# The expert layers of a two-block transformer on one core: 96 of 256 tokens by row gathers, the other 160 by dense plain-float32 matmuls

## The reference, cut to what matters

```python
def block(xc):                                   # 128 tokens; 8 heads, top 16 of 128 x 128 experts each
    q = (xc @ w_q).reshape(128, 8, 2, 128)
    sc = einsum('thpd,hpnd->thpn', q, subkeys)
    s1, i1 = top_k(sc[:, :, 0], 16); s2, i2 = top_k(sc[:, :, 1], 16)
    top, pos = top_k(all 256 sums s1 + s2, 16)
    idx = (i1 * 128 + i2 at pos)                  # 128 experts a token
    gate = softmax(top)
    act = gelu(einsum('ted,td->te', u[idx], xc))
    return einsum('te,ted->td', gate * act, v[idx])
x = layer_norm(ALPHA * x + peer_ffn(x, ...), ...)
```

## Time and profile before

| | us |
|---|---|
| median of 3 runs | 2287.73 (2286.67 to 2289.21) |
| span of the profiled execution | 2284.1 |
| TensorE busy in it | 2268.4 (99%) |
| VectorE, ScalarE, GpSimd busy | 1699.0, 1324.8, 430.5 |
| moved by DMA | 408.53 MB, mean 179 GB/s |

### The profile page before, as it was taken

How to read it: one execution, slowest core, us unless ns; L and a number is a source line. 1 busy time by engine, 2 the same in 40 slices (tenths; PEclk the granted TensorE clock), 3 DMA queues, 4 the chain that set the end, 5 groups by cost and what they waited for, 6 DMA issues and landing times.

```text
span 2284.1 us, 33324 instructions
## 1 busy us (share of the span) xinstructions
PE 2268.4 (99%) x12380; PEld 1929.4 (84%) x12380; DVE 1699.0 (74%) x3098; ACT 1324.8 (58%) x2181; POOL 430.5 (19%) x355
## 2 busy tenths in 40 slices
PE   9999999999999999999999999999999999999999
PEld 9788888888888888887788888888888888877887
DVE  7567588999975555668758898997555666877885
ACT  3454555578765554646555558776555564666554
POOL 1000233178710000000013316872000000000000
PEclk9999999999999999999999999999999999999999
DMA  7455455544455655644455554445556575333555
GB/s 257 156 176 190 161 191 189 183 167 156 149 194 193 203 193 194 231 163 142 141 171 187 193 177 169 153 155 190 194 193 232 184 227 179 135 123 118 185 186 173
DMA packets 112096, 408.53 MB, mean 179 GB/s; under 512 B 12592, under 2 KB 12640, under 8 KB 111680
## 3 DMA queue, kind: packets, MB, share of 16 engines
q1 hardware_dynamic: 107712, 391.63, 50.4%
q0 software_dynamic: 3504, 13.47, 1.7%
q10 hardware_dynamic: 720, 1.31, 0.2%
HBM read 405.30 MB, written 1.05 MB: 178 GB/s over the span
## 4 chain that ended last, share of the span: by engine, by line
PE 87%; DVE 9%; ACT 2%; issue 1%; DMA 1%; POOL 0%; ACTq 0%; DVEq 0%
PE ps L716 24%; PE ps L633 21%; PE ps L705 12%; PE ps L636 11%; PE ps L672 3%; PE ps L669 3%; PE ps L676 3%; DVE lo L1967 3%; PE ps L915 2%; PE ps L768 1%; DVE big L1973 1%; ACT hi L1373 1%; DVE big L2303 1%; PE ps L889 1%; PE ps L616 1%
## 5 line engine op out<-in xcount | busy, mean ns | idle before, releaser
L1967 DVE TENSOR_TENSOR lo<-raw,hi 128x1024 fp32r<-128x1024 f32 (+1 forms) x627 | 765.4, 1224 | 366.1 <-ACT hi L1373 363.6
L1373 ACT ACTIVATE hi<-raw 128x1024 fp32r<-128x1024 f32 x677 | 714.3, 1057 | 479.7 <-PE ps L716 270.7
L633 PE MATMUL ps<-xs,hi 128*128 128x512 f32 x2560 | 650.8, 396 | 1.0 <-DVE big L2918 1.0
L633 PEld LDWEIGHTS ps<-xs,hi 128*128 128x128 f32 x2560 | 459.2, 189 | 83.6 <-DVE big L2918 1.1
L636 PEld LDWEIGHTS ps<-xs,lo 128*128 128x128 f32 x2560 | 349.0, 190 | 25.8
L636 PE MATMUL ps<-xs,lo 128*128 128x256 f32 x2560 | 356.3, 282 | 0.0
L2998 POOL TENSOR_SCALAR lnp<-iota,selT 128x128 f32<-128x128 f32 x256 | 278.1, 1097 | 167.0 <-DVE negT L2345 88.9
L705 PE MATMUL ps<-hi,lefts 128*128 128x512 f32 x986 | 304.0, 389 | 0.0
L716 PE MATMUL ps<-lo,lefts 128*128 128x512 f32 x986 | 303.7, 389 | 0.0
L716 PE MATMUL ps<-hi,lefts 128*128 128x512 f32 x986 | 303.6, 389 | 0.0
L716 PEld LDWEIGHTS ps<-hi,lefts 128*128 128x128 f32 x986 | 184.9, 188 | 38.7 <-DVE lefts L2033 0.2
(11 more groups left out here) (370 smaller groups left out, 2505.8 us busy)
## 6 DMA issues: line engine op xcount, KB each, us to landing
raw<-in_peer_u SPq DMA_DIRECT2D x256, 512.0 KB, 3.2
raw<-in_peer_v SPq DMA_DIRECT2D x256, 512.0 KB, 4.2
raw<-in_ret_vg SPq DMA_DIRECT2D x32, 512.0 KB, 3.2
raw<-in_peer_q SPq DMA_DIRECT2D x24, 512.0 KB, 3.2
raw<-in_ffn_up SPq DMA_DIRECT2D x22, 512.0 KB, 3.3
raw<-in_ffn_down SPq DMA_DIRECT2D x22, 512.0 KB, 4.0
raw<-in_ffn_gate SPq DMA_DIRECT2D x18, 512.0 KB, 4.3
raw<-in_ret_qk SPq DMA_DIRECT2D x16, 512.0 KB, 4.6
```

Source lines behind the costliest of these rows:

```text
L633: e.matmul(out, uh[:, k, :], xs[:, k, :, :].rearrange("p h t -> p (h t)"), start=k == 0, stop=False)
L1373: e.activation(parts(i)[0][:, 0:w], raw[:, i % N_RAW, 0:w], ACT.Copy).then_inc(s_hi, 1)
L1967: e.tensor_tensor(ul[:, 0:w], raw[:, i % N_RAW, 0:w], uh[:, 0:w].bitcast(F32), ALU.subtract).then_inc(s_lo, 1)
```

## The change

96 tokens (0 to 95) are looked up. The selection of tile 0 yields `listed`, the 128 row numbers of each token. POOL copies it so that two experts of tokens 0 to 63 (64 lists), and four of tokens 64 to 95 (32 lists), stand on the 128 partitions, and gathers for each list 128 rows of 4 KB, 512 KB a gather, into one of six buffers `rows`; 96 gathers from each table and layer. DVE multiplies and sums a gathered tile with copies of `x` (first table) or adds it, weighted, into `sums` (second table); two small matmuls with `fold` bring `sums` back to tokens.

The other 160 tokens are dense, in plain float32 and unsplit, in both halves. A unit lands in one of six buffers `plain`, which lie where `hi` and `lo` lay, and is the weights of 8 matmuls with 160 columns. The second table's result comes out turned (features by tokens) and is turned back at the end. Splits, halves and adds of these units fall away. The selection is taken at 15 steps a unit and is due at c = 20, gates are spread in 40 groups from c = 22, the looks begin at c = 8.

```diff
+LOOKED = 96
+DENSE = S - LOOKED
+GROUPS = DENSE // 4
+N_PLAIN, N_ROWS, LATE = 6, 6, 6
+YIELDS, LISTED, SPREAD, LOOKS = 15, 20, 22, 8
+PAIRS, FOURTHS = 64, 32
+LISTS = PAIRS + FOURTHS
 def peer_schedule():
-            if c >= 36:
-                turns += 1
-                n = 2 if turns % 4 == 0 else 1
+            n = 1 if c >= SPREAD and (2 * (c - SPREAD) + j) % 2 == 0 else 0
+            steps[c, j] = list(range(at, min(at + n, GROUPS + 2)))
+            gathers += [q + N_ROWS] * len(steps[c, j])
+            n = 1 if c >= LOOKS and (2 * (c - LOOKS) + j) % 5 < 4 and q < LISTS else 0
+            looks[c, j] = list(range(q, q + n))
+    for k in range(128):
+        n = min(2 * LISTS - q, 1)
...
 # PE, first table
-                    for j in range(2):
-                        feat_wide(n + j, u.view[:, j, :], X_PEER[l])
+                    for j in range(2):
+                        m = 256 * l + 2 * c + j
+                        w = plain[:, m % N_PLAIN, :].rearrange("p (k n) -> p k n", k=8)
+                        e.wait_ge(*plain_landed(m))
+                        for k in range(8):
+                            ins = e.matmul(u.view[:, j * DENSE:(j + 1) * DENSE], w[:, k, :], Peer.xT[:, k, :],
+                                           start=k == 0, stop=k == 7)
+                        ins.then_inc(s_pused, 1)
-                    if c == 34:
+                    if c == LISTED:
                         for t in range(2):
                             e.wait_ge(s_gate, 2 * l + t + 1)
                             turn(("selT", l, t), LOWER, ...)
-                acc(f"peer_v{l}", 128, after=after, tail=6, between=between)
+                second_weights(l, after)
+            def second_weights(l, after):
+                e.wait_ge(*use["G", l, GROUPS - 1].freed)
+                def blocks(k, first):
+                    w = plain[:, (256 * l + 128 + k) % N_PLAIN, :]
+                    for b in range(4 * first, 8 if first or k < 128 - LATE else 4):
+                        ins = e.matmul(us[b // 2].view[:, b % 2 * DENSE:(b % 2 + 1) * DENSE],
+                                       w[:, b * 128:(b + 1) * 128], experts[:, k, :], ...)
+                for k in range(128):
+                    if k == 128 - LATE:
+                        e.wait_ge(*looked(l, 2 * LISTS))
+                        e.wait_ge(s_fold, 16 * (l + 1))
+                        for f in range(2):
+                            for i in range(2):
+                                e.matmul(ys[f].view, Peer.fold[:, 128 * i:128 * i + 128],
+                                         Peer.sums[i][:, f * 512:(f + 1) * 512], start=i == 0, stop=False)
+                    e.wait_ge(*plain_landed(256 * l + 128 + k))
+                    ins = blocks(k, 0)
+                for k in range(128 - LATE, 128):
+                    blocks(k, 1).then_inc(s_pused, 1)
+                    if k == 124:
+                        turn_back(0)
+                turn_back(1)
-            peer(0, 0, between=lambda j: xs_tile(X_DIFF, xk, normed_x(1), 0) if j == 4 else None)
+            peer(0, 0)
+            xs_tile(X_DIFF, xk, normed_x(1), 0)
...
 # DVE
-                            for _ in range(5 + (j and c % 2)):
+                            for _ in range(YIELDS):
                                 next(steps, None)
+                def look(q):
+                    e.wait_ge(*rows_landed(l, q))
+                    w = Peer.act[:, i:i + 1]
+                    if q < LISTS:
+                        e.tensor_tensor_reduce(rows, rows, copies, 1.0, 0.0, ALU.mult, ALU.add, w).then_inc(s_looked, 1)
+                        return
+                    e.wait_ge(*looked(l, q))
+                    if i in (0, PAIRS):
+                        e.tensor_scalar(sums, rows, w, None, ALU.mult).then_inc(s_looked, 1)
+                    else:
+                        e.scalar_tensor_tensor(out=sums, in0=rows, scalar=w, in1=sums, op0=ALU.mult,
+                                               op1=ALU.add).then_inc(s_looked, 1)
...
 # POOL
+            def look_up(l, q):
+                if q >= N_ROWS:
+                    e.wait_ge(*looked(l, q - N_ROWS + 1))
+                e.indirect_dma_start(out=Peer.rows[m % N_ROWS], out_offset=None, in_=table,
+                                     in_offset=bass.IndirectOffsetOnAxis(ap=Peer.idx[:, i:i + 1], axis=0)
+                                     ).then_inc(s_row[m % N_ROWS], 16)
-                for i in POOL_UNITS:
-                    low_part(W.first[f"peer_u{l}"] + i)
-                for i in range(64):
+                for i in range(GROUPS):
+                    while q < GATHERS[i]:
+                        look_up(l, q)
+                        q += 1
                     build(l, i)
+                for q in range(q, 2 * LISTS):
+                    look_up(l, q)
...
 # SP
+            def plain_load(l, i):
+                m = 256 * l + i
+                if i < N_PLAIN:
+                    e.wait_ge(s_used, split_before[m] + 1)
+                else:
+                    e.wait_ge(*plain_used(l, i - N_PLAIN + 1))
+                e.dma_start(plain[:, m % N_PLAIN, :], src).then_inc(s_plain[m % N_PLAIN], 16)
```

More of the change, by code:

```diff
@@ L436, in build @@
             sel = [several(R, 3, 8, 16), several(R, 3, 8, 16)]
-            keys = region(big, 14848)(2, UNIT)
+            listed = R(128, dt=U32)
+            R = region(big, 22528)
+            xT = R(8, DENSE)
+            copies = sums = several(R, 2, UNIT)
+            rows = several(R, N_ROWS, UNIT)
+            keys = region(big, 30080)(2, UNIT)
+            idx, act, gate = R(LISTS, dt=U32), R(LISTS), R(LISTS)
+            yT = region(big, 22528)(8, 128), region(big, 8704)(8, 128)
+            fold = selT.rearrange("p s t -> p (s t)")[:, 0:256]
             oha = [lnp[:, s, 0:512].rearrange("p (u n) -> p u n", u=4) for s in range(2)]
@@ L567, in build @@
         place(W.first["peer_q1"] + 3, First.query[1], (s_scored, 16))
[L568 to L575, removed]
         for i in range(3):
-            place(W.first["diff_q0"] + i, Tail.more[1 + i], *read("peer_v0", 128))
+            place(W.first["diff_k0"] + i, Tail.w[i], plain_used(0, 128 + -(-(4096, 15872, 17920)[i] // DENSE)))
+        place(W.first["diff_k0"] + 3, Tail.more[0], looked(0, 2 * LISTS), plain_used(0, 256 - LATE + 1))
+        for i in range(3):
+            place(W.first["diff_q0"] + i, Tail.more[1 + i], looked(0, 2 * LISTS), plain_used(0, 256 - LATE + 1))
         for i in range(4):
@@ L581, in build @@
             place(W.first["diff_w_out"] + 6 + i, Diff.late[i], (s_scored, 16))
-        place(W.first["w_in_c"] + 3, Tail.more[0], *read("peer_v1", 128))
+        for i in range(3):
+            place(W.first["xa_w_kv"] + i, Tail.keys[i], plain_used(1, 128 + -(-(9856 + 2048 * (i + 1)) // DENSE)))
+        place(W.first["w_in_c"] + 3, Tail.more[0], looked(1, 2 * LISTS), plain_used(1, 256))
         for i in range(3):
@@ L1389, in feat_units @@
                 for j in range(n):
[L1390 removed]
+                    n = W.first[stage] + first + j + 2
+                    hi_to(min(n, W.first[stage] + 15) if stage in ("peer_q0", "peer_q1") else n)
                     if step:
@@ L2259, in topk, with peer, plain_xT @@
                                     ALU.subtract).then_inc(s_sel, 1)
+                    if t == 0:
+                        first, second = (a.rearrange("p h k -> p (h k)") for a in Peer.sel[0][0:2])
+                        e.scalar_tensor_tensor(out=Peer.listed, in0=first, scalar=128.0, in1=second, op0=ALU.mult,
+                                               op1=ALU.add).then_inc(s_idx, 1)
                     yield
-            def peer(l, norms, after=None, more=0):
+            def peer(l, norms, ahead, after=None):
                 n0 = W.first[f"peer_q{l}"]
+                def plain_xT(t):
+                    cut, mine = ((slice(LOOKED, 128), slice(0, 128 - LOOKED)), (slice(0, 128), slice(128 - LOOKED, DENSE)))[t]
+                    for g in range(2):
+                        v = use["xs", X_PEER[l], t, g].view.rearrange("p (k t) -> p k t", k=4)
+                        e.tensor_copy(Peer.xT[:, 4 * g:4 * g + 4, mine], v[:, :, cut]).then_inc(s_xt, 1)
                 for _ in norms[0]:
@@ L3009, in beside_experts @@
-                for i in range(64):
-                    build(l, i)
-                e.wait_ge(*use["u", l, 63].freed)
-                ln_load(l, 1)
+                copies(l)
+                e.wait_ge(s_idx, l + 1)
+                pairs_out(Peer.idx, Peer.listed, s_list)
+                e.wait_ge(s_list, 96 * l + 32)
+                early = N_ROWS + sum(len(LOOKS_AT[c, j]) for c in range(LISTED) for j in range(2))
+                for q in range(early):
+                    look_up(l, q)
@@ L3052, in pool @@
             e.dma_start(Sec.ukv, A["mla_ukv"][0]).then_inc(s_mla, 16)
-            e.wait_ge(s_used, used("peer_v1", 127))
+            for i in range(4):
```

(1 more changed line is left out.)

370 lines of the change are left out of this document (253 added, 117 removed).

## The result

The changed kernel takes 2162.97 us (median of 4 runs, 2160.89 to 2164.10), the kernel before 2287.44 (4 runs, 2286.67 to 2289.21): a ratio of 0.9455, 95% interval 0.9442 to 0.9469. The forecast was 2150.

The account below looks back on a forecast made before the run. It took TensorE, 99% busy, as the bound. Layer 0 summed 129 + 213 + 328 + 11 = 681 us and layer 1 674, saving 138 of 2284.1; with 3.6 from span to median, 2150, range 2060 to 2265.

Parts of the forecast that it names:

- TensorE's new work: In the experts: dense float32 units of 2.18 us; TensorE alone 590 us against 747, saving 157 a layer.
- Stage A: From unit 0 to the end of c = 20: 129 us a layer, TensorE waiting 32 for the gates.
- The 2 us for the clock: At c = 20, behind TensorE's wait for the gates: 2 us added because its clock falls after idle time.
- Stage B: Rest of the first table behind c = 20, 86 units: 213 us, POOL's chunk 4.2 against TensorE's 4.90.
- DMA: Gathers and dense transfers together at 405 GB/s, 1.29 us per 512 KB; a second-table unit with a gather 2.59 us.
- Rival 2: DMA slower in long stages, 350 GB/s, 1.50 us a transfer: total 2266; chance 0.23 including anything else between 2195 and 2283.
- rival 1: DMA carries both streams without loss, 419 GB/s or more, and POOL is never late: total 2062; chance 0.12.
- Stages C and D: Second table with gathers, 249 us, and without, 70; with border, fold and turning back 328 in all.
- The end of layer 0: Behind layer 0's experts: the bare chain from first addition to split, 9.2 us, and 2 for the clock; 11 charged.
- costed at nothing: ACT's lighter load, small DMAs on POOL, first plain units' buffer wait and splits ahead for the next stage: no time charged.
- Rival 3: In POOL's queue from c = 20, a gather holds POOL 3 us: 106 us a layer more, total 2362; chance 0.15.

Follow-up runs that it names:

- e3: e2 with the looks beginning at c = 20 instead of c = 8; 2110.40 us, ratio 0.9222.
- e5: Changed kernel with first-table gathers, but for a layer's first six, bringing 512 bytes a row instead of 4096; 2168.79 us, ratio 0.9475.
- e6: Changed kernel with three small memsets, each waited for, on POOL ahead of gathers 32 to 95 of the first table; 2220.33 us, ratio 0.9703.
- e8: Changed kernel with the edits of e2 and e1, and a look in every unit from c = 20 instead of four of five; 2110.21 us.
- e4: Changed kernel with the second table's gathers bringing 512 bytes a row instead of 4096; 2067.91 us, ratio 0.9038.
- e2: Changed kernel with splits of four next-stage units moved behind the first copy of layer 0's turned result; 2153.46 us, ratio 0.9411.
- e1: Changed kernel with POOL issuing the next stage's constants behind gather 60 of the second table instead of 30; 2148.11 us, ratio 0.9382.

## Why the prediction was right, step by step

- **TensorE's new work: right.** A unit is 2.18 us, as scaled by columns from the key scores, and a chunk with a spread group 4.86 (4.90 forecast). The saving of 157 us a layer rests on this term, and no other was near it in size.
- **Stage A: 124.4 and 125.1 us, forecast 129.** The selection alone takes 96.2 (e3) where I had 6.6 + 93 + 2 = 101.6. Its offset is 6.6 as forecast (its first step starts at 265.45), so the 5.4 too many lie in the 93 and the 2. The looks cost 26.7 where I had 25, and that is partly luck: the units 16 to 39, four of five, are 20 and not 19, each took 1.15 and not 1.3, and the 3.8 us of waiting for rows made up for it. The wait is 26.9 and 27.5, forecast 32. The 2 us for the clock held: behind the wait the granted clock was 0.50, its low level of 1.2 GHz, until 386 and full from 388, and the first 80 records took 12.91 us where in e3, without a wait, they took 11.03.

```profile
384.00:386.00 2.00, 2.00 (x9) 2.00 (x9) 1.86 (x8) 0.00 (x0) 2.00 (x5) 0.50 0.97 356
...
388.00:390.00 2.00, 2.00 (x17) 2.00 (x17) 2.00 (x5) 0.35 (x2) 0.07 (x1) 1.00 0.80 242
```
- **Stage B: 211.8 and 214.0, forecast 213**, but with wrong parts. A gather took POOL 1.16 and 0.27 between issues, 1.43 together (1.3 forecast); a build 2.46 (2.1 forecast). POOL's chunk was 1.6 x 1.43 + 2.46 = 4.75 us, not 4.2, against TensorE's 4.86: it was much nearer to being the bound than I wrote, and in e5, e6 and e8 it is one. The sum of the stage came out by luck, since TensorE stayed 0.1 us a chunk ahead of what was mis-sized. POOL by lines in 386 to 595 us gives both prices, and the 8.0 us that it waited for a look, all its slack:

```profile
L3168 POOL TENSOR_SCALAR lnp<-iota,selT 128x128 f32<-128x128 f32 x80 | 98.4, 1236 | 1.6
L3179 POOL DMA_INDIRECT big<-in_peer_ur,big x69 | 80.2, 1163 | 26.3 <-issue 18.3 <-DVE big L2495 8.0
```

- **DMA: right.** The 405 GB/s from windows of 4 us turned out 409 over 70 us at a share of 1.03. In the steady second table looks follow each other every 2.56 us, two transfers of 1.28 (1.29 forecast). The Trainium skill's page "DMA: Bandwidth & Descriptors", section "Specifications", has about 358 GB/s for a core; the trace does not agree with it. Rival 2, and the 2242 worked out from that figure, died by this row, and so did rival 1, which wanted 481 GB/s. e4 comes near rival 1's 2062 (2068), for a second table without DMA's limit.
- **Stages C and D: 333.3 us in layer 0, forecast 328.** Without the 6.7 us of e2 it is 326.6.
- **The end of layer 0: 10.4 us from DVE's first addition (928.84 to 939.2), forecast 11.** In layer 1 I had 4, and the keys start 2.6 us behind the last dense matmul.
- **Wrong: "costed at nothing".** It named the small DMAs on POOL, each an issue of 0.54, behind six gathers in flight, and the splits ahead on ACT and DVE. The issues are 0.6 each, as said. But the step failed in asking what they cost and not what they wait for. In layer 1 the constants wait 47 us for TensorE in POOL's queue, ahead of 65 gathers; the six buffers cover 16 us. DMA falls to 279 GB/s, all later looks come late, and DVE's norm of the memory rows (L2740) stands in DVE's order behind late looks while TensorE waits for it: 15 us (e1). In layer 0 the same pause (34.8 us) ends in no wait of TensorE. The splits cost 6.7 to 9.5 us by DVE's order (e2). The two together are more than the 13 us between 2150 and 2162.97; the savings in A, about 4 a layer, gave 8 back. By layer: layer 0 came out at 680.3 against 681, which is luck, since what was too much in A hid the 6.7; layer 1 at 686.8 against 674, which is the miss. About 3 us more lie outside the experts.
- **Rival 3: refuted.** A gather alone took 0.94 us and 0.30 to the next. Beside DVE's looks most took 1.01 to 1.09 and some 1.93; the longest of all in the experts took 2.00.

```profile
1701.64 1.08 POOL L3179 DMA_INDIRECT big<-in_peer_v,big  x1 [0.30 <-issue]
...
1704.70 1.93 POOL L3179 DMA_INDIRECT big<-in_peer_v,big  x1 [0.65 <-DVE big L2501]
```

That is twice at most. The Trainium skill's page "SBUF — State Buffer", section "SBUF: two separate sides", has five times for a whole transfer beside DVE in a two-port mode; these rows are the issue on POOL, and show no such factor. Whether the looks run in such a mode, and what makes some issues long, no run here tells.

## What to carry to other kernels

A wait in an in-order queue costs what stands behind it, so a "small DMA" is priced by its condition and not by its issue. When a change fills a resource that was half idle, look for each pause in its feeding, since it can no longer catch up: the same pause was free where the bytes were fewer (e4) and cost 15 us here. And where look-ups can be put anywhere, put them where no engine is yet late: the same 20 looks cost 27 us bare beside the selection, and about 9 in the DMA-bound stretch (8 to 13, by what it is compared with).

## What the runs showed of the hardware

- Gathers of 128 rows of 4 KB, together with plain transfers of 512 KB, ran at 409 GB/s; I had found no row for them and had taken them as equal to dense ones. They are.
- GpSimd's float32 operation on 128 x 128 went from 1.04 to 1.34 us in the same line between kernels (e6, e5), its indirect issue from 0.94 to 2.00 in the changed kernel. A price of its queue read in one place did not hold in another.
- TensorE was granted 0.55 of full speed, so nearly its low level of 1.2 GHz, over 29 us of which it stood idle for the gates in 26.9. It was still at 0.50 when work began again, and back at 1.00 some 6 us later.
